# Convolution layer in another order, pairs read by halves, products nobody reads, and one root for a double norm

## The chip, the cores and the metric

The kernel runs on 1 core of one Trainium2 chip. The metric is the device time of one execution in microseconds, the median of the runs shown. It was measured three times before the change.

## The reference, cut to what matters

A residual stream x of 256 tokens by 1024 features (fp32) goes through six layers, each a mixer and a feed-forward part, with an RMS norm ahead of each of them:

```python
for i in range(4):                       # retention, conformer convolution, stick breaking, retention
    x = x + mixer_i(rms_norm(x, norm_mix[i]))
    x = x + squared_relu_mlp(rms_norm(x, norm_ffn[i]), ffn_w1[i], ffn_w2[i])
x = rms_norm(x, final_norm)              # together with the next one: a double norm
for layer in range(2):                   # hybrid layers
    h = rms_norm(x, g_mix[layer])
    ...
return rms_norm(x, g_final)
```

The convolution mixer is `h = a * sigmoid(gate)` from one projection, a causal depthwise convolution of 31 taps over time for each of the 1024 channels, a layer norm over the channels, silu, and a projection. The retention mixer projects q, k, v and a gate; q and k are normed over each head of 256 features, rotated, and used for decayed scores over the 256 tokens. `rms_norm(x, w) = x * rsqrt(mean(x*x) + 1e-6) * w`.

## The kernel before, in words

Weights stream through two buffers of 2 MB ("units" of 128 x 4096 fp32, loaded by SyncE in two pieces of 1 MB; unit u is loaded when unit u-1 has been split). ScalarE rounds each piece to fp32r (`w_hi`, L1327), VectorE takes the rest (`w_lo`, L1926), and TensorE makes every product of three: high by high, high by low, low by high (`three`, L778 to L780; `unit_both`, L807 and L810, does it in two). The activations (`act_hi`, `act_lo`, `hid_hi`, `hid_lo`) are split in the same way. Every engine walks the same list of units in an order written out by hand, and semaphores tie the engines together.

Results go to two PSUM `pair`s of 1024 columns (two banks each), used in turn: `open_pair` waits until the use before the last was drained, by ScalarE or VectorE, which signal `drained`. The residual sums of the output projections go to a third PSUM region, `acc`.

**Retention** (`retention` on each engine). Four units make q and k by tokens (`unit_t`: the product of tokens 0 to 127 into the pair's first bank, of tokens 128 to 255 into its second; each unit has two pieces, so the first bank is complete at three quarters of the unit). ScalarE copies the whole pair (L1549), takes four sums of squares (L1553), evacuates the turned pair before (`rotate_evac`, L1544), takes the root (`roots`); VectorE norms and rotates (L2199 to L2210) and signals `qk_ready`; TensorE turns the result (`transposes`, L944). Per head a unit makes v, which ScalarE copies whole into `R_V` (L1570), scores (L1003) follow, then a gate unit, and the weighted sum (L1011 to L1013).

**Convolution layer** (`conformer`). Four units give h; ScalarE adds biases and takes the sigmoid (L1597, L1600), VectorE multiplies two tiles of 128 channels each (`gated(i)`, L2321, which signals `conv_gated`). Tiles 0 and 1 are convolved on VectorE, 31 taps by two tiles, 62 instructions (L2301, L2304), with the other work of VectorE put between them by `between`. Tiles 2 to 7 (`STACKED_TILES`) are convolved on TensorE (`convolve(n)`, L1029, 32 products each, in four groups of 32 columns) from copies shifted in time: GpSimd (`stack_tiles`) stores two tiles of h to `u_rows` in HBM (L669), waits for the landing, and gathers each tile back with four DMAs (L676) into one of four buffers. Tiles 6 and 7 use the buffers of tiles 2 and 3 again, so GpSimd waits for `squared` before it gathers them. The channel mean is first estimated from tiles 0 and 1 (`C_NEG`, L1042 on TensorE, L1624 on ScalarE) and taken off every tile (L2346, L2331); the exact mean and variance come by products with `C_MEAN` (L1047 to L1055), the last of which need tile 7. L1639, L1640, L2364, L1642 and L2371 to L2376 make the normed values, L1651 the silu, L1385 and L1979 the split, and the output projection starts (`unit_r`, L778).

```python
gated(0)
convolve(0, 1, {4: second_piece, 14: lambda: gated(1), 15: lambda: ahead(CONV_FIRST + 3), 27: lambda: gated(2)})
gated(3)
```

**Norms** (`norm`, on ScalarE and VectorE). Per half a of the tokens and half n of the columns VectorE adds the residual (L2014), multiplies by the gain row (`by_row`, L2006), ScalarE squares with a running sum (L1417), VectorE adds and inverts (L2020, L2021), ScalarE takes the root (L1400) and scales (L1406), TensorE turns the half (`turn_half`, L848), inside the first unit for a = 1. Ahead of hybrid layer 0 (`row=True`) the norm is double: after the first root ScalarE writes x back, normed with the row `final_norm` (L1406, `x<-work`), then the second gain, the second sum, the second root and the second scaling follow for the same half.

**Start and end.** At the start x, the identity and the first weights are loaded, normed (`norm_first`) and turned. At the end VectorE scales each half of the tokens (L2740), and GpSimd stores it as one DMA of 512 KB (L736).

## Time and profile before

| what | value |
|---|---|
| median of 3 runs | 2360.89 us (2360.59 to 2361.51) |
| the profiled execution, its own time | 2362.6 us |
| its span, first to last instruction | 2360.8 us |
| mean granted TensorE clock in it | 0.996 |
| HBM read, written | 430.73 MB, 6.16 MB; 185 GB/s over the span |

The rows further down are from the profiled execution, in microseconds from its first instruction. A timeline row reads: start, duration, engine, line, operation, output <- input, shape, count, and in brackets how long the engine had been idle before it and what released it. Ends of matmuls are modelled (a matmul's duration holds its way through the array), so the pace of TensorE is read from start to start. Equal instructions that follow each other are merged into one row with a count.

### The profile page before, as it was taken

How to read it: one execution, taken by the hardware profiler on the slowest of the kernel's cores; microseconds unless marked ns; L12 is line 12 of the kernel's file. 1: busy time of each engine (PE TensorE's matmuls, PEld its weight loads, DVE VectorE, ACT ScalarE, POOL GpSimd, SP SyncE). 2: the span in 40 equal slices, each digit the busy share in tenths (PEclk: the TensorE clock that was granted, in tenths of full speed). 3: DMA queues.
4: the chain of work that ended last, by engine and by line, in shares of the span. 5: the costliest groups of instructions: out<-in, count | busy, mean ns of one | idle time of the engine just before them, and what ended most of it. 6: DMA issues, size and time to landing. Idle time of an engine off the chain costs nothing.

```text
span 2360.8 us, 31036 instructions
## 1 busy us (share of the span) xinstructions
PE 2311.3 (98%) x12362; PEld 1933.3 (82%) x12362; DVE 1571.2 (67%) x1650; ACT 1211.9 (51%) x1347; POOL 86.1 (4%) x136
## 2 busy tenths in 40 slices
PE   8999999889999999999999999999999999999998
PEld 6788888678888788877788877888888887888887
DVE  7666676766567765686576567867655667677555
ACT  5545445354356644464454365544644656446444
POOL 0000030200000000000000000000000000000000
PEclk9999999999999999999999999999999999999999
DMA  7454654634443355545454544445454544454543
GB/s 272 185 173 178 246 201 191 203 112 188 187 179 155 139 199 213 196 161 191 183 201 178 189 176 176 168 161 200 180 196 178 216 178 173 161 192 182 197 174 128
DMA packets 71848, 434.21 MB, mean 184 GB/s; under 512 B 11648, under 2 KB 11968, under 8 KB 26176
## 3 DMA queue, kind: packets, MB, share of 16 engines
q1 hardware_dynamic: 59184, 399.78, 44.2%
q0 software_dynamic: 12560, 32.96, 4.5%
q8 instruction: 75, 1.23, 0.2%
q14 instruction: 29, 0.24, 0.0%
HBM read 430.73 MB, written 6.16 MB: 185 GB/s over the span
## 4 chain that ended last, share of the span: by engine, by line
PE 93%; DVE 4%; ACT 2%; issue 1%; DMA 0%; POOL 0%; DVEq 0%; ACTq 0%
PE pair L807 21%; PE pair L810 11%; PE acc L778 10%; PE acc L779 10%; PE acc L780 10%; PE pair L778 6%; PE pair L780 5%; PE pair L779 5%; PE pair L819 4%; PE pair L820 2%; PE pair L1029 1%; DVE work L2304 1%; DVE w_lo L1926 1%; PE pair L848 1%; PE acc L1206 1%
## 5 line engine op out<-in xcount | busy, mean ns | idle before, releaser
L1926 DVE TENSOR_TENSOR w_lo<-raw,w_hi 128x2048 fp32r<-128x2048 f32 (+1 forms) x402 | 865.0, 2173 | 112.4 <-ACT w_hi L1327 108.6
L1327 ACT ACTIVATE w_hi<-raw 128x2048 fp32r<-128x2048 f32 (+1 forms) x402 | 717.0, 1805 | 53.7 <-PE acc L780 47.9
L807 PE MATMUL pair<-act,w_hi 128*128 128x512 f32 x1920 | 602.7, 395 | 0.0
L810 PEld LDWEIGHTS pair<-act,w_lo 128*128 128x128 f32 x1920 | 360.6, 188 | 84.8
L810 PE MATMUL pair<-act,w_lo 128*128 128x256 f32 x1920 | 377.3, 278 | 0.0
L778 PE MATMUL acc<-w_hi,hid 128*128 128x512 f32 x848 | 333.9, 394 | 0.0
L779 PE MATMUL acc<-w_lo,hid 128*128 128x512 f32 x848 | 330.4, 390 | 0.0
L780 PE MATMUL acc<-w_hi,hid 128*128 128x512 f32 x848 | 330.2, 389 | 0.0
L807 PEld LDWEIGHTS pair<-act,w_hi 128*128 128x128 f32 x1920 | 295.5, 189 | 3.6
L1472 ACT ACTIVATE gate<-pair 128x512 f32<-128x512 f32 x104 | 62.2, 598 | 458.2 <-PE pair L810 435.8
L2116 DVE TENSOR_TENSOR gate<-pair,gate 128x512 f32<-128x512 f32 x104 | 71.7, 690 | 255.0 <-ACT gate L1472 254.6
L778 PE MATMUL pair<-w_hi,act 128*128 128x512 f32 (+1 forms) x576 | 228.0, 396 | 5.1 <-DVE act L1979 2.7
L780 PE MATMUL pair<-w_hi,act 128*128 128x512 f32 (+1 forms) x576 | 222.2, 386 | 0.0
L779 PE MATMUL pair<-w_lo,act 128*128 128x512 f32 (+1 forms) x576 | 222.1, 386 | 0.0
L780 PEld LDWEIGHTS acc<-w_hi,hid 128*128 128x128 f32 x848 | 159.2, 188 | 33.6
L778 PEld LDWEIGHTS acc<-w_hi,hid 128*128 128x128 f32 x848 | 159.2, 188 | 33.2 <-issue 1.9
L779 PEld LDWEIGHTS acc<-w_lo,hid 128*128 128x128 f32 x848 | 159.2, 188 | 32.0 <-issue 1.4
L819 PE MATMUL pair<-act,w_hi 128*128 128x512 f32 x448 | 162.2, 403 | 0.0
L778 PEld LDWEIGHTS pair<-w_hi,act 128*128 128x128 f32 x576 | 108.8, 189 | 32.5 <-issue 9.5
L780 PEld LDWEIGHTS pair<-w_hi,act 128*128 128x128 f32 x576 | 108.7, 189 | 22.1
L779 PEld LDWEIGHTS pair<-w_lo,act 128*128 128x128 f32 x576 | 108.8, 189 | 20.6 <-issue 0.7
L820 PE MATMUL pair<-act,w_lo 128*128 128x256 f32 x448 | 125.5, 280 | 0.0
(273 smaller groups left out, 2671.9 us busy)
## 6 DMA issues: line engine op xcount, KB each, us to landing
raw<-weights SPq DMA_DIRECT2D x354, 1024.0 KB, 6.7
raw<-weights SPq DMA_DIRECT2D x52, 512.0 KB, 4.0
work<-bias_scratch POOLq DMA_DIRECT2D x32, 192.0 KB, 2.7
val<-gains POOLq DMA_DIRECT2D x11, 512.0 KB, 4.0
bias_scratch<-bias_rows POOLq DMA_DIRECT2D x4, 1024.0 KB, 19.9
hid<-u_rows POOLq DMA_DIRECT2D x20, 142.0 KB, 3.4
work<-ret_gn_w POOLq DMA_DIRECT2D x8, 256.0 KB, 5.3
work<-ret_gn_b POOLq DMA_DIRECT2D x8, 256.0 KB, 5.8
```

The lines of the kernel that those rows point to most:

```text
L778: mm(o, a_hi, b_hi, start=start, stop=False)
L779: mm(o, a_hi, b_lo, start=False, stop=False)
L780: return mm(o, a_lo, b_hi, start=False, stop=stop)
L807: mm(tiles(o[:, 512 * n:512 * n + 512]), h[:, k, n * P:(n + 1) * P], both[:, :, k, :], start=k == 0, stop=False)
L810: last = mm(o[:, 512 * n:512 * n + SEQ], l[:, k, n * P:(n + 1) * P], both[:, 0, k, :], start=False, stop=k == KT - 1)
L819: mm(tiles(o[:, b:b + 512]), h[:, k, cs], both[:, :, k, :], start=k == 0, stop=False)
L820: last = mm(o[:, b:b + SEQ], l[:, k, cs], both[:, 0, k, :], start=False, stop=k == KT - 1)
L848: last = tr(o[:, P * k:P * (k + 1)], xs[:, a, P * k:P * (k + 1)], ident[:])
L1327: run(w_hi[slot][:, part], raw[slot][:, part], ACT.Copy).then_inc(hi_done, 1)
L1472: run(tiles(dst), o[:].rearrange("p (n h t) -> p n h t", n=2, h=2)[:, :, 1, :], ACT.Copy).then_inc(gate_ready, 1)
L1926: tt(w_lo[slot][:, part], raw[slot][:, part], w_hi[slot][:, part].bitcast(F32), ALU.subtract).then_inc(lo_done, 1)
L2116: return tt(tiles(dst), o[:].rearrange("p (n h t) -> p n h t", n=2, h=2)[:, :, 0, :], tiles(low), ALU.add).then_inc(done, 1)
```

## The change

It has five parts.

1. Retention: `unit_t` and `first_unit` signal `token_half` when the first bank of the pair is complete. ScalarE copies that bank (and, for q and k, squares it) then, and the second bank after the unit. `roots(4)` comes ahead of `rotate_evac(i - 1)`. The v pairs are copied in the same two halves.
2. Convolution layer: `gated(1)`, the split of unit `CONV_FIRST + 3`, `gated(2)` and `gated(3)` stand at taps 6, 9, 14 and 28 of VectorE's convolution (before: 14, 15, 27 and behind it). The split of unit `CONV_FIRST + 4` comes behind the convolution, not ahead of `gated(3)`. TensorE convolves tiles 2, 3 and 4 at once, takes the mean estimate from tiles 2 and 3, and then convolves tiles 5, 6 and 7; ScalarE evacuates tiles 2 to 4 with their bias; `C_NEG` is taken off five tiles in one instruction. GpSimd waits for `drained` in place of `squared`. Tile 6 enters the exact mean by the sum on VectorE. `C_DSQ` is made ahead of `C_DELTA`, and VectorE waits for it alone.
3. Products that nobody reads (`keep_busy`, fp32, 128x128x128, into a part of `acc` that is written anew afterwards): 18 ahead of the first load's wait, 12 behind the first turn, 24 behind the last variance product of the convolution layer.
4. Double norm: `both_inverses` gives both roots at once from two sums of squares: with s1 the mean square of x and s2 that of x*row, the first root is 1/sqrt(s1+eps), both together 1/sqrt(eps*(s1+eps)+s2). The gain is multiplied on at once; x itself is scaled at the end of `norm` on VectorE.
5. End: VectorE scales the first 512 columns, ScalarE the other 512, and SyncE stores each quarter (256 KB) as soon as it is ready, in place of two DMAs of GpSimd.

The diff, cut to its core:

```diff
@@ sync @@
+            for a in range(2):
+                for n in range(2):
+                    sp.wait_ge(out_ready[n], a + 1)
+                    sp.dma_start(out[P * a:P * (a + 1), wide(n)], xs[:, a, wide(n)]).then_inc(out_stored, 16)
+            sp.wait_ge(out_stored, 64)
@@ gpsimd @@
                         if n >= 4:
-                            pool.wait_ge(squared, n - 2)
+                            p = CONV_PAIR + n - 4
+                            pool.wait_ge(drained[p % 2], p // 2 + 1)
...
-            for a in range(2):
-                pool.wait_ge(x_ready, x_signals - 3 + 3 * a)
-                pool.dma_start(out[P * a:P * (a + 1), :], xs[:, a, :]).then_inc(stored, 16)
-            pool.wait_ge(stored, 112)
@@ tensor @@
+                        if by_half and (piece, a) == (1, 0):
+                            last.then_inc(token_half, 1)
...
+            def keep_busy(m, n):
+                for _ in range(n):
+                    mm(IDLE, m, m, start=True, stop=True)
...
-                pe.wait_ge(conv_ready, 2)
+                uses = [convolve(n) for n in range(3)]
+                assert uses[0] == CONV_PAIR
+                await_drained(uses[1])
                 o = open_pair()
-                for k in range(2):
-                    last = mm(o[:, 0:SEQ], C_MEAN, C_Y[:, k, :], start=k == 0, stop=k == 1)
+                for k in (2, 3):
+                    last = mm(o[:, 0:SEQ], C_MEAN, C_Y[:, k, :], start=k == 2, stop=k == 3)
                 last.then_inc(pair_full, 1)
-                uses = [convolve(n) for n in range(len(STACKED_TILES))]
+                uses += [convolve(n) for n in range(3, 6)]
                 o = open_pair()
                 pe.wait_ge(summed, 1)
...
-                for k in (6, 7):
-                    await_drained(uses[k - 2])
...
+                await_drained(uses[5])
+                mm(o[:, 0:SEQ], C_MEAN, C_Y[:, 7, :], start=False, stop=True).then_inc(mean_ready, 1)
+                pe.wait_ge(squared, 4)
+                mm(o[:, 512:512 + SEQ], C_MEAN, C_SQ[:, 7, :], start=False, stop=True).then_inc(pair_full, 1)
+                keep_busy(ident[:], 24)
...
+            pe.wait_ge(warm_in, 1)
+            keep_busy(WARM, 18)
             pe.wait_ge(loaded, 16)
             first_half()
+            keep_busy(ident[:], 12)
@@ scalar, norm @@
                     if row:
-                        times_root(a, x, x_ready)
+                        for n in range(2):
+                            square_of(x, a, n, 2 * a + n)
+                            last = square_of(BY_ROW, a, n, 4 + 2 * a + n)
+                        last.then_inc(ss_ready, 1)
+                        act.wait_ge(rinv_ready, S.due("rinv_ready"))
+                        link(run(rstd[:, 2 * a:2 * a + 2], rinv[:, 2 * a:2 * a + 2], ACT.Sqrt))
+                        for n in range(2):
+                            run(xs[:, a, wide(n)], xs[:, a, wide(n)], ACT.Copy,
+                                scale=rstd[:, 2 * a:2 * a + 1]).then_inc(xs_ready, 1)
+                    else:
                         square(a, 0)
                         square(a, 1)
-                    times_root(a, xs, xs_ready)
+                        times_root(a, xs, xs_ready)
@@ scalar, retention @@
                 for i in range(4):
-                    next_unit()
+                    ahead(S.u + 1)
                     o, done, slot = use()
-                    run(xs[:, i % 2, :], o[:], ACT.Copy).then_inc(done, 1)
...
+                    for a in range(2):
+                        if a == 0:
+                            await_half()
+                            link(run(xs[:, i % 2, wide(a)], o[:, wide(a)], ACT.Copy))
+                        else:
+                            unit_end()
+                            run(xs[:, i % 2, wide(a)], o[:, wide(a)], ACT.Copy).then_inc(done, 1)
+                            await_drained(S.p - 1)
+                        for g in (2 * a, 2 * a + 1):
...
                     last.then_inc(ss_ready, 1)
+                    roots(4)
                     if i:
                         rotate_evac(i - 1)
-                    roots(4)
@@ scalar, conformer @@
+                for k in (2, 3, 4):
+                    o, done, _ = use(False)
+                    await_pair()
+                    run(C_Y[:, k, :], o[:, 0:SEQ], ACT.Identity, bias=colv("dw_b", k)).then_inc(done, 1)
...
+                square(0, 5)
+                for k in (5, 6, 7):
                     use(False)
                     await_drained(S.p - 1)
                     square(k)
+                    if k < 7:
+                        split_piece(S.u + 1, k - 5)
...
+                run(C_DSQ, o[:, 0:SEQ], ACT.Square).then_inc(delta_ready, 1)
                 run(C_DELTA, o[:, 0:SEQ], ACT.Copy).then_inc(delta_ready, 1)
@@ scalar, end @@
+                root(a).then_inc(last_root, 1)
+                act.wait_ge(last_root, a + 1)
+                run(xs[:, a, wide(1)], xs[:, a, wide(1)], ACT.Copy, scale=rstd[:, a:a + 1]).then_inc(out_ready[1], 1)
@@ vector @@
+            def both_inverses(a):
+                whole, first = rinv[:, 2 * a:2 * a + 1], rinv[:, 2 * a + 1:2 * a + 2]
+                dve.wait_ge(ss_ready, S.due("ss_ready"))
+                link(stt(first, ss[:, 2 * a:2 * a + 1], EPS, ss[:, 2 * a + 1:2 * a + 2], ALU.add, ALU.add))
+                link(stt(whole, first, EPS, ss[:, 4 + 2 * a:5 + 2 * a], ALU.mult, ALU.add))
+                link(tt(whole, whole, ss[:, 5 + 2 * a:6 + 2 * a], ALU.add))
+                nc.vector.reciprocal(rinv[:, 2 * a:2 * a + 2], rinv[:, 2 * a:2 * a + 2]).then_inc(rinv_ready, 1)
...
+                            tt(BY_ROW[:, a, wide(n)], x[:, a, wide(n)], ROW[:, wide(n)], ALU.mult).then_inc(x_ready, 1)
+                            dve.wait_ge(x_ready, S.due("x_ready"))
+                            by_row(a, n, gain, BY_ROW)
...
+                if row:
+                    for a in range(2):
+                        link(ts(x[:, a, :], BY_ROW[:, a, :], rstd[:, 2 * a + 1:2 * a + 2], None, ALU.mult))
@@ vector, conformer @@
                 gated(0)
-                convolve(0, 1, {4: second_piece, 14: lambda: gated(1), 15: lambda: ahead(CONV_FIRST + 3),
-                                27: lambda: gated(2)})
-                gated(3)
+                convolve(0, 1, {4: second_piece, 6: lambda: gated(1), 9: lambda: ahead(CONV_FIRST + 3),
+                                14: lambda: gated(2), 28: lambda: gated(3)})
+                ahead(CONV_FIRST + 4)
...
+                five_y = C_Y[:, 0:5, :]
+                tt(five_y, five_y, C_NEG.unsqueeze(1).broadcast_to([P, 5, SEQ]), ALU.add).then_inc(centred, 1)
...
                 o, done = fetch_pair()
-                dve.wait_ge(delta_ready, 2)
+                dve.wait_ge(delta_ready, 1)
@@ vector, start and end @@
+            nc.vector.memset(WARM, 0.0).then_inc(warm_in, 1)
...
-                await_roots()
-                ts(xs[:, a, :], xs[:, a, :], rstd[:, a:a + 1], None, ALU.mult).then_inc(x_ready, 1)
+                dve.wait_ge(last_root, a + 1)
+                ts(xs[:, a, wide(0)], xs[:, a, wide(0)], rstd[:, a:a + 1], None, ALU.mult).then_inc(out_ready[0], 1)
```

## Rows read from the trace of the kernel before

**Rows 1.** The page, busy time of the engines: us, share, instructions.
```profile
PE 2311.3 (98%) x12362; PEld 1933.3 (82%) x12362; DVE 1571.2 (67%) x1650; ACT 1211.9 (51%) x1347; POOL 86.1 (4%) x136
```

**Rows 2.** The waits of PE: line waited, releaser: us in total, times, longest.
```profile
PE acc L778 <- DVE act L1979: 6.4, 1, 6.4
...
PE pair L1003 <- ACT work L1570: 3.9, 8, 1.2
```

**Rows 3.** Timeline of PE in retention 0: start, us, instruction, xcount [idle before <-releaser].
```profile
36.04 1.03 PE L944 MATMUL pair<-ident,work 128*128 128x128 f32 x8
37.31 0.50 PE L778 MATMUL pair<-w_hi,act 128*128 128x512 f32 x1 [0.24 <-ACT work L1549]
...
70.35 0.39 PE L780 MATMUL pair<-w_hi,act 128*128 128x512 f32 x1
70.83 1.09 PE L944 MATMUL pair<-ident,work 128*128 128x128 f32 x8
71.67 0.48 PE L778 MATMUL pair<-w_hi,act 128*128 128x512 f32 x1
```

**Rows 4.** Chain that ended last: start, us, what.
```profile
61.19 1.03 ACT work L1549
```

**Rows 5.** Groups by form, ACT, 444 to 494: busy, mean ns, idle.
```profile
L1385 ACT ACTIVATE act<-val 128x512 fp32r<-128x512 f32 x4 | 2.5, 630 | 0.1
```

**Rows 6.** Timeline of DVE in the convolution layer.
```profile
435.05 9.59 DVE L2304 SCALAR_TENSOR_TENSOR work<-work,cols 128x256 f32<-128x256 f32 x24
...
448.45 4.49 DVE L1926 TENSOR_TENSOR w_lo<-raw,w_hi 128x2048 fp32r<-128x2048 f32 x2
452.86 0.69 DVE L2321 TENSOR_TENSOR work<-work,gate 128x512 f32<-128x512 f32 x1
```

**Rows 7.** Timeline of PE in the convolution layer.
```profile
433.08 0.35 PE L778 MATMUL pair<-act,w_hi 128*128 128x256 f32 x1 [0.73 <-DVE w_lo L1926]
...
448.59 1.91 PE L1042 MATMUL pair<-work 128*128 128x256 f32 x4 [3.77 <-DVE work L2304]
...
461.68 3.63 PE L1029 MATMUL pair<-val,work 128*32 128x256 f32 x64
...
469.60 8.61 PE L1029 MATMUL pair<-hid,work 128*32 128x256 f32 x128 [4.29 <-issue]
...
479.97 0.59 PE L1051 MATMUL pair<-work 128*128 128x256 f32 x2
...
480.40 0.59 PE L1055 MATMUL pair<-work 128*128 128x256 f32 x2
...
487.35 0.77 PE L778 MATMUL acc<-w_hi,act 128*128 128x512 f32 x1 [6.35 <-DVE act L1979]
```

**Rows 8.** One line's view, L669, the three stores of u_rows.
```profile
DMA to landing us min/median/max: 2.9/3.2/9.9
```

**Rows 9.** Windows: length, busy PE PEld DVE ACT POOL, clock, DMA share, GB/s.
```profile
488.00:492.00 4.00, 4.00 (x11) 3.17 (x10) 3.21 (x5) 3.94 (x10) 0.00 (x0) 0.50 0.00 0
...
500.00:510.00 10.00, 10.00 (x46) 8.24 (x45) 7.58 (x9) 6.05 (x9) 0.00 (x0) 1.00 0.47 199
```

**Rows 10.** Timelines of ACT and PE, double norm before hybrid layer 0.
```profile
1385.07 1.34 ACT L1406 ACTIVATE x<-work,small 128x512 f32<-128x512 f32 x2
...
1388.29 1.33 ACT L1406 ACTIVATE work<-work,small 128x512 f32<-128x512 f32 x2
...
1389.07 0.66 PE L848 MATMUL pair<-ident,work 128*128 128x128 f32 x4 [2.28 <-ACT work L1406]
```

**Rows 11.** Timeline of PE at the start.
```profile
11.43 0.76 PE L778 MATMUL pair<-w_hi,act 128*128 128x512 f32 x1 [2.69 <-DVE act L1979]
...
15.37 0.40 PE L778 MATMUL pair<-w_hi,act 128*128 128x512 f32 x1
```

**Rows 12.** Timelines of DVE and POOL at the end.
```profile
2354.59 0.75 DVE L2740 TENSOR_SCALAR work<-work,small 128x1024 f32<-128x1024 f32 x1 [0.27 <-ACT small L1400]
...
2355.64 0.54 POOL L736 DMA_DIRECT2D out<-work  x1 [3.56 <-DVE work L2740]
```

116 lines of the change are left out of this document (58 added, 58 removed).

## The prediction

> **What bounds the kernel now.** I read the page first: TensorE is busy 98% of the span [rows 1], so apart from fewer products only its waits and its half-speed stretches can be won. TensorE's waits come next [rows 2], then the timeline around each. They fall into five places, one for each part of the change. Durations are from the profiled execution (2362.6 us, span 2360.8); its own time is 1.7 above the median of the runs, 2360.89, and I take the sum off the median.
>
> **Retention, by halves.** After a unit TensorE turns the rotated pair before, and then needs the pair that ScalarE is copying. From the start of the turn to the next product are 1.27 us where it waits (36.04 to 37.31) and 0.84 where it doesn't (70.83 to 71.67) [rows 3]: 0.43 is lost, though the idle column says 0.24. The copy of 1024 columns takes 1.03 [rows 4], one of 512 0.63 (the nearest form, also out of PSUM) [rows 5]. With the first bank copied during the unit's last quarter, the pair is free 0.40 earlier, just about when the turn is through. There are five such places for q and k (the row at 37.31 is the first), and eight for v, where TensorE waits 3.9 in all [rows 2]: two of them wait 1.21, and keep 0.8. So 13 x 0.40 = 5.2. `qk_ready` is late too: the product at 70.35 should be followed after 0.23 but the turn starts 0.48 later [rows 3]; now the squares of the first bank lie under the unit, and the sums are ready over 1 us earlier. 2 x 0.25 = 0.5. Sum 5.7. What the part adds: an extra fixed cost of two ScalarE copies per unit (2 x 0.63 against 1.03, so 0.2) and a wait at three quarters of the unit; behind that wait on ScalarE stands only what before stood behind the end of the unit, since the split of the next unit comes ahead of both. `rotate_evac` slips about 0.8 behind the root, and is needed a unit later. Bounds: 0 (ScalarE reading one bank slows the products into the other; nothing here shows it) and 6.5.
>
> **Convolution layer.** Before: the fourth unit ends at 444.8 (448.59 less 3.77), TensorE waits for VectorE's last tap, makes the mean estimate, convolves four tiles, waits 4.29 for the gathered tiles, and starts the output projection at 487.35 [rows 7].
> VectorE first. A tap instruction takes 0.40 (9.59 for 24), a split pair 4.4 (448.45 to 452.86) [rows 6]. VectorE has no gap here, so positions can be shifted by sums: the last `gated` moves ahead of six taps (2.4) and of a split pair (4.4), from 452.86 to 446.1. `gated(2)` moves from tap 27 to 14, to about 434.5. The last tap ends at 449.2, the split pair at 453.6. The split that made TensorE wait 0.73 at 433.08 [rows 7] now comes ahead, five taps earlier: the unit ends 0.8 earlier, at 444.0.
> TensorE: a tile takes 3.5 at full clock (3.63 for tile 5, modelled end included). Tiles 2 to 4: 444.0 to 454.5, two mean products of 0.43 (479.97 to 480.40) to 455.4, tiles 5 to 7 to 465.9 [rows 7].
> Is what it needs there? `C_NEG` at 456, five tiles at once on VectorE (some 1.5) and three sums to about 459.3, the squares' sums to 461.5: tile 5's drain at 459.4 comes 3 us ahead of tile 7's need of that pair. `summed` is made near 464, ahead of 465.9. The third store is issued at 446.9 rather than 453.8. The three stores landed after 2.9, 3.2 and 9.9 us [rows 8]; the slow one went out just behind 2 MB of weights. At 446.9 the weights of the unit before have landed and the next are asked for at 453.6, so I take 3.2: gathers from 450.2, one per 0.55, the last at 454.1. With about 3.5 to land they are there by 457.6, against 462.4 when tile 7 needs its buffer. The weights then in flight touch only the last gather.
> The end: four statistics products to 467.7; the projection starts 6.5 behind their end before (480.83 to 487.35), now 6.2, as the squares are made first: 473.9. That is 13.4 earlier than 487.35.
> The clock: from 488 to 492 it is granted at 0.50, 1.2 GHz, with 11 records (nine starts) in 4 us; later 1.00, 2.4 GHz, with 46 in 10 us (0.227 each) [rows 9]. It had fallen in the 6.35 us of idleness before 487.35. The 24 dummy products are 128 columns, half of 0.43, so 0.22 each: 5.2 us, from 467.7 to 472.9, a microsecond ahead of need. So they cost nothing, and the idleness left is 1 us. At half speed from 487.35 to at least 492, at most 494, half of it was lost: 2.3 to 3.3, I take 2.8. Sum 13.4 + 2.8 = 16.2. Bounds: 11 (a stall of up to 5, below) and 17.5.
>
> **A rule against the trace.** The weights ride on SyncE's queue, the stores and gathers on GpSimd's, and the third store took three times as long beside weights [rows 8]. The Trainium skill, "DMA: Bandwidth & Descriptors", section "SWDGE vs HWDGE vs iDMA", says that a DMA engine goes round robin between such queues, by which a store of 0.3 MB would get its share beside the weights and land long before them. By that rule no placement here costs a stall, and the last two gathers are safe; the row says otherwise, and I keep the stall as a rival.
>
> **Double norm.** ScalarE's first scaling starts at 1385.07, the second at 1388.29, and TensorE's turn follows at 1389.07 after 2.28 of idleness [rows 10]. The pass between the scalings, 3.2 us, goes. The new chain adds per half a product (0.69), a square (0.6) and two tiny instructions (0.4); but VectorE, rid of the second pass of a = 0, starts a = 1's residual 1.1 us earlier, and the first product of the unit comes 1.1 earlier too. My walk has the second turn at 1385.9, 3.2 earlier, with 0.5 of idleness left. The scaling of x at the end (2 x 0.75, the price of L2740 [rows 12]) delays the split behind it by 0.6 against its cover, ScalarE's rounding; TensorE needs that split 0.7 later. If that cover were gone it would cost 0.6. I take 3.2; bounds 2 and 4.
>
> **Start.** The first product runs at 11.43, and until 15.37 products start 0.43 apart instead of 0.23 [rows 11], the pace of the half clock. The 18 dummies start at about 1.0, at half speed at first, and end between 6.4 and 7.7; the first turn was at 6.8. At full clock the first products outrun VectorE's splits, which then gate them: my walk gives 0.7. Bounds: a loss of 1 (the dummies delay the turn) and a gain of 1.5.
> The Trainium skill, "TensorE: Matmul & The Clock Gate", Part 1, says that the number of slow products at a kernel's start differs from run to run; by it the same 18 would sometimes be too many, within those bounds.
>
> **End.** The last scaling starts at 2354.59 and takes 0.75, GpSimd's issue follows at 2355.64 [rows 12]. Halves on two engines save 0.3 for a = 0 and 0.1 for a = 1, and SyncE can issue without the 0.3 that lay between the scaling (ended 2355.34) and GpSimd's row: 0.7. Bounds: 0 and 2, since a smaller last store may also land sooner. The skill's DMA page above, "Anatomy of one DMA", has 2.0 us fixed plus the bytes at 436 GB/s, an estimate of 0.6 less for 256 KB than for 512; by it the sum would be 0.6 lower.
>
> **Sum.** 5.7 + 16.2 + 3.2 + 0.7 + 0.7 = 26.5; 2360.9 - 26.5 = 2334.4. Behind these places the MLP stages are all TensorE, and VectorE's splits run ahead there, so what is won stays won.
>
> **Rivals.**
> *The clock doesn't hold* (the dummies are too few or come too late): the 2.8 and the start's 0.7 are gone, 2337.9. For it: the half clock held 4 us and more under real work [rows 9]. Against it: only 1 us of idleness is left. 0.12.
> *The gathers stall*: the third store lands as late as before (9.9): gathers from 456.9 to 460.8, tile 6 waits 3.6, and the clock may fall once more, 1.7: 2339.7. For it: rows 8. Against it: no weights in flight at 446.9. 0.15.
> *The halves give nothing*: ScalarE reading beside TensorE's writes, or coming late to its wait: 2340.1. 0.08.
> *Slower than before*: the clock falls ahead of the layer's convolutions, and their short products of 32 columns don't bring it back, so that 21 us of tiles, 2.6 of statistics, 5.2 of dummies and 21.8 of projection all take twice as long, 50 us more: 2384. It decides once more than 26.5 us of full-speed work runs at half speed. Against it: tiles 6 and 7, 6.9 us at full clock, took 8.6 after a gap of 4.29 [rows 7], so these products do bring the clock back. 0.03.
> *The change doesn't do what it says* in its largest part: no such case, the order is written out.
>
> **The numbers.** As forecast 0.62, its own range 2331 to 2337. The range for 8 in 10 takes in clock and gathers: 2330 to 2340. A measurement of this kernel can tell about 0.2%, 4.7 us. Faster by more 0.95, within it 0.02, slower 0.03.
>
> **What would show it.** Right: TensorE's waits on L1549 and L1570 shrunk to two of about 0.8; tile 5, 6 and 7 without a gap; a granted clock of 1.00 through the projection; one wait of about 0.5 at the double norm. Wrong: an idle time of over 1 us ahead of tile 6 or 7, 0.50 behind the dummies, the dummies ending later than VectorE's first `act_lo`, or the first turn later than 6.8.

## The result, and the profile after

The changed kernel takes 2347.39 us (median of 4 runs, 2345.64 to 2349.41), against 2361.2 for the kernel before on the same chip: a ratio of 0.9937, 95% interval 0.9922 to 0.9952. It is faster by 13.8 us; 26.5 were forecast, and the time lies outside the range. The sign was right, the size was off by half, and most of what is missing is in one place.

The two profiled executions (spans 2360.8 and 2346.5) differ by 14.3 us. The table reads them stage by stage, as the shift of the same instruction between the two timelines of TensorE. The forecast for retention, 5.7 for both layers, is split by its places: 2.65 in retention 0 and 3.05 in retention 1.

| part | forecast | found |
|---|---|---|
| start and retention 0 (last turn before the layer: 411.16, now 410.87) | 3.35 | 0.29 |
| convolution layer, start of its projection (487.35, now 484.38) | 13.4 | 2.68 |
| the clock behind it (projection to the next norm's product: 204.90, now 202.45) | 2.8 | 2.45 |
| retention 1 | 3.05 | 2.38 |
| double norm | 3.2 | 3.64 |
| end (start of the last product to the end of the span: 10.12, now 7.26) | 0.7 | 2.86 |
| sum | 26.5 | 14.3 |

The page's busy times, which answer to [rows 1]. TensorE now stands for 29 us of its span instead of 50. It has 104 records more: 108 of the products that nobody reads (54, two records each), less 4 of the statistics, so part of the busy time is theirs:

```profile
PE 2317.8 (99%) x12466; PEld 1943.3 (83%) x12466; DVE 1571.9 (67%) x1654; ACT 1215.9 (52%) x1359; POOL 85.4 (4%) x134
```

The waits of TensorE (line waited for, us in total, times, longest), against [rows 2]. The wait of 6.4 ahead of the projection is gone, and the eight for the v pair (now L1023) are two of 0.8, as forecast. At the head stands a wait that was 4.3 before: the taps (now L1049), released by "issue", that is, by nothing that the engines' records name.

```profile
PE pair L1049 <- issue: 7.8, 2, 6.8
...
PE pair L1023 <- ACT work L1618: 1.6, 2, 0.8
PE pair L789 <- DVE w_lo L1977: 1.5, 2, 1.2
PE pair L789 <- DVE w_lo L2094: 1.2, 1, 1.2
```

Where it stands shows in the timeline of TensorE in the convolution layer, against [rows 7]. Everything that the engines do runs as forecast: tile 2 at 443.51 (forecast 444.0), no wait for the mean estimate, and 6.37 us from the end of the last statistics product to the projection (forecast 6.2). But tile 4 waits 1.06 and tile 6 waits 6.78:

```profile
443.51 7.11 PE L1049 MATMUL pair<-hid,work 128*32 128x256 f32 x128
451.68 3.66 PE L1049 MATMUL pair<-hid,work 128*32 128x256 f32 x64 [1.06 <-issue]
...
466.77 9.48 PE L1049 MATMUL pair<-hid,work 128*32 128x256 f32 x128 [6.78 <-issue]
...
478.01 5.52 PE L859 MATMUL acc<-ident 128*128 128x128 f32 x48
484.38 0.47 PE L789 MATMUL acc<-w_hi,act 128*128 128x512 f32 x1 [0.85 <-DVE act L2030]
```

The wait of 6.78 costs more than itself. Tiles 6 and 7 then take 9.4 us (466.77 to the first statistics product at 476.18) where they need 7.0 at full clock (a tile is 3.47 from start to start, 453.63 to 457.10 in hold_all below). The windows of 2 us show the granted clock (busy PE with its records, clock, DMA share, GB/s): half at first, full later. That is another 2.4 us.

```profile
468.00:470.00 2.00, 2.00 (x24) 0.50 0.00 0
474.00:476.00 2.00, 2.00 (x44) 1.00 0.00 0
```

Tiles 4 and 6 wait for gathers, so the next view is GpSimd's queue in the same stretch. VectorE had the second and third pairs gated at 434.7 and 446.5. The second store goes out at once, at 435.07, but GpSimd then waits 10.38 us for it to land. The third store stands in the same queue behind that wait and behind eight gathers, and goes out at 450.52, not at 446.9:

```profile
423.48 0.74 POOL L683 DMA_DIRECT2D u_rows<-work  x1 [65.25 <-DVE work L2390]
430.10 4.39 POOL L691 DMA_DIRECT2D hid<-u_rows  x8 [5.88 <-DMA u_rows<-work]
435.07 0.72 POOL L683 DMA_DIRECT2D u_rows<-work  x1 [0.57 <-DVE work L2390]
446.17 2.19 POOL L691 DMA_DIRECT2D hid<-u_rows  x4 [10.38 <-DMA u_rows<-work]
448.35 2.18 POOL L691 DMA_DIRECT2D val<-u_rows  x4
450.52 0.72 POOL L683 DMA_DIRECT2D u_rows<-work  x1
455.35 0.57 POOL L691 DMA_DIRECT2D hid<-u_rows  x1 [4.10 <-DMA u_rows<-work]
```

What lay beside it is on SyncE: the weight loads, two DMAs of 1 MB each time, issued when the unit before has been split. The change also moved one of them, since the split of unit `CONV_FIRST + 3` now stands at tap 9 and not at 15: VectorE is through with it at 430.09 instead of 435.13. The load that went out at 435.32 before goes out at 430.27; the one after it stays (453.40, before 452.97). SyncE before, then after:

```profile
435.32 0.86 SPq L556 DMA_DIRECT2D raw<-weights  x2
```

```profile
430.27 0.86 SPq L565 DMA_DIRECT2D raw<-weights  x2
...
453.40 0.82 SPq L565 DMA_DIRECT2D raw<-weights  x2
```

The time from issue to landing, the three stores (L683) and then the 24 gathers (L691), against [rows 8]:

```profile
DMA to landing us min/median/max: 4.5/6.3/10.8
```

```profile
DMA to landing us min/median/max: 3.1/8.0/11.1
```

Before, they were 2.9/3.2/9.9 and 2.7/3.5/9.6. The order of time says more. The eight gathers issued from 430.10, beside the load of 430.27, take 5.2 to 11.1; the eight from 446.17, with no weights in flight, 3.1 to 3.9; the eight from 455.35, beside the load of 453.40, 7.6 to 9.4. The stores take 6.3, 10.8 and 4.5. Before the change five gathers took over 5 us, now sixteen do.

In retention 0, VectorE's first head norm waits 4.84 us for a table that it doesn't use (2.69 before, when TensorE had no wait behind it); TensorE now waits twice, 1.96 in all. These are the rows of VectorE and TensorE:

```profile
29.84 0.17 DVE L2041 TENSOR_SCALAR small<-small 128x4 f32<-128x4 f32 x1 [4.84 <-DMA work<-table_bucket_hot]
...
36.33 1.09 PE L964 MATMUL pair<-ident,work 128*128 128x128 f32 x8 [0.76 <-DVE work L2278]
38.62 0.47 PE L789 MATMUL pair<-w_hi,act 128*128 128x512 f32 x1 [1.20 <-DVE w_lo L1977]
```

The double norm on TensorE, against [rows 10]: the wait of 2.28 ahead of the second turn is 0.17, and from the start of the unit's last product (1370.29, before 1378.15) to the second turn there are 7.42 us instead of 10.92. The other wait in this stretch, ahead of the unit's first product, is 1.62 and was 1.90.

```profile
1370.52 1.03 PE L866 MATMUL pair<-ident,work 128*128 128x128 f32 x8
1373.18 0.47 PE L789 MATMUL acc<-w_hi,act 128*128 128x512 f32 x1 [1.62 <-issue]
...
1377.71 0.66 PE L866 MATMUL pair<-ident,work 128*128 128x128 f32 x4 [0.17 <-ACT work L1496]
```

The end, against [rows 12], VectorE and then SyncE. The last scaling takes 0.49, and a quarter store lands 2.2 us after its issue, where half the output took 2.9:

```profile
2342.88 0.49 DVE L2814 TENSOR_SCALAR work<-work,small 128x512 f32<-128x512 f32 x1 [0.27 <-ACT small L1422]
...
2339.57 4.64 SPq L609 DMA_DIRECT2D out<-work  x4
```

### The profile page after: what moved, and what is told of

Read it like the earlier page. It is cut to its first block, busy times and chain, and to the rows that moved or that the text cites. A ratio compares the mean times of both kernels' runs of the same rounds, so it can differ in the third digit from the quotient of the medians.

```text
span 2346.5 us, 31261 instructions
## 1 busy us (share of the span) xinstructions
PE 2317.8 (99%) x12466; PEld 1943.3 (83%) x12466; DVE 1571.9 (67%) x1654; ACT 1215.9 (52%) x1359; POOL 85.4 (4%) x134
## 4 chain that ended last, share of the span: by engine, by line
PE 93%; DVE 3%; ACT 1%; DMA 1%; issue 1%; SPq 0%; POOL 0%; DVEq 0%; ACTq 0%; POOLq 0%
PE pair L818 22%; PE pair L821 11%; PE acc L789 10%; PE acc L790 10%; PE acc L791 10%; PE pair L789 6%; PE pair L791 5%; PE pair L790 5%; PE pair L830 4%; PE pair L831 2%; DVE w_lo L1977 1%; PE pair L1049 1%; PE pair L964 1%; PE pair L866 1%; PE acc L1225 1%
## 5 line engine op out<-in xcount | busy, mean ns | idle before, releaser
L1507 ACT ACTIVATE gate<-pair 128x512 f32<-128x512 f32 x104 | 62.2, 598 | 457.6 <-PE pair L821 435.4
```

What stands on the lines that cost most here:

```text
L1507: run(tiles(dst), o[:].rearrange("p (n h t) -> p n h t", n=2, h=2)[:, :, 1, :], ACT.Copy).then_inc(gate_ready, 1)
```

## Experiments

The theory after this reading: the convolution layer's gain is eaten by weight loads that share the DMA engines with stores and gathers; hold them back and the forecast's timeline comes true. Rivals: the order in GpSimd's queue (the third store stands behind the second's gathers), or a fixed price of these transfers when they start early. All kernels below are the changed kernel with one edit, unless said otherwise. A view used throughout is the distance from tile 2 to the projection: 36.91 before, 40.87 after, 29.9 in the forecast (444.0 to 473.9).

**hold_both.** The weight loads are held at two places: one until the second store has landed, the next until all gathers have.

```diff
+                if mixer_units == 6:
+                    loads(4)
+                    load()
+                    sp.wait_ge(u_stored, 32)
+                    load()
+                    sp.wait_ge(stacked[1], 128)
+                else:
+                    loads(mixer_units)
```

> The changed kernel, but SyncE issues the sixth unit's load of the convolution layer (at 430.3 in the changed kernel) only when the second store of u_rows has landed, and the load after it (453.4) only when tile 7 is gathered. Theory (weights in flight beside GpSimd's stores and gathers make them late): the second store lands in about 3 us instead of 11, the third goes out at about 446 instead of 450.5, tile 4 waits less than 1, tiles 6 and 7 wait at most 1, the projection starts at 474 to 477 instead of 484.4, and the time is 8 to 11 us below the changed kernel (2336 to 2340). Rival (the stores and gathers are slow by themselves, small packets through GpSimd's queue): the gap of 6.8 ahead of tile 6 stays over 5, the time stays at 2345 to 2349. A second rival (the held loads come too late for the next units): a new wait for w_lo of 2 us or more behind the layer.

Measured: 2340.75 us, ratio to the kernel before 0.9908 (0.9892 to 0.9925), a little outside the 2336 to 2340 expected. The distance falls from 40.87 to 34.80. Stores land after 4.2/6.2/8.1 us: the third, issued at 445.69, ran beside the weights released at 438.18, and tile 6 still waits 2.34 where at most 1 was expected. Holding the load earns 6.1 of the 11 us, and where a load was let go too early, the store beside it was slow again.

**third_store_first.** GpSimd issues the third store ahead of the second store's gathers; the loads are untouched.

```diff
...
+                    if i == 2:
+                        store(3)
+                    if i == 3:
+                        pool.wait_ge(third_stored, 16)
...
```

> The changed kernel, but GpSimd stores the third pair of tiles as soon as the second store has landed and the tiles are ready (about 446.5), ahead of the eight gathers of tiles 4 and 5, not behind them (450.5). Loads are not held. Theory (GpSimd's own order makes the third store late, 4 us of the gap): store at 446.5, gathers of tiles 6 and 7 from about 451, the gap of 6.8 ahead of tile 6 falls to 1 to 3.5; tile 4 waits 0.7 longer. Time 3 to 5 us below the changed kernel. Rival (only the weights issued at 453.4 count): the gathers of tile 7 still run beside them and land when they land, the gap moves to tile 7 and the time falls by under 2.

Measured: 2343.88 us (0.9926, 0.9909 to 0.9942). The store goes out at 444.94, and the wait of 6.78 ahead of tile 6 becomes three waits, here in TensorE's timeline:

```profile
451.49 3.66 PE L1057 MATMUL pair<-hid,work 128*32 128x256 f32 x64 [2.95 <-issue]
...
460.14 3.66 PE L1057 MATMUL pair<-hid,work 128*32 128x256 f32 x64 [0.34 <-issue]
466.33 5.57 PE L1057 MATMUL pair<-hid,work 128*32 128x256 f32 x64 [2.53 <-issue]
```

5.82 together instead of 7.84, and a distance of 38.61. The queue's order is worth about 2 us here, and it isn't clear of the spread: the executions whose loads and stores are those of the changed kernel lie between 37.9 and 41.7, and the intervals of the two ratios overlap. The larger part, by the run above, is the weights'.

**hold_all.** One hold, but for everything: the load that went out at 430.27, and with it the one behind, waits until tile 7 is gathered.

```diff
+                if mixer_units == 6:
+                    loads(4)
+                    load()
+                    sp.wait_ge(stacked[1], 128)
+                    load()
+                else:
+                    loads(mixer_units)
```

> The changed kernel, but both loads that ran beside the stores and gathers (the sixth unit's and the one behind it) are issued only when tile 7 is gathered. In the run that held the sixth only until the second store had landed, the third store still took 8.1 us beside it. Theory (each store and gather beside weights is slow, alone it takes about 3 to 4): the third store goes out at about 446 and lands in 3 to 4 us, tile 6 waits under 0.5 us, and from tile 2's first product to the projection's first are 29.5 to 31 us (40.9 in the changed kernel, 34.8 with the earlier hold); time 2335 to 2338. Against it (GpSimd's own queue is the limit): 33 to 35 us from tile 2 to the projection, as with the earlier hold. The sixth unit then arrives at about 463, which ScalarE's splits between the squares may feel: at most 2 us.

Measured: 2338.04 us (2336.09 to 2339.21; 0.9892, 0.9876 to 0.9909), 9 us below the changed kernel. The distance is 33.25, more than the 29.5 to 31 expected and in the range that was to speak for GpSimd's queue as the limit. Where the time goes decides between them. Stores and gathers from issue to landing:

```profile
DMA to landing us min/median/max: 3.0/4.2/6.2
```

```profile
DMA to landing us min/median/max: 2.7/3.3/4.7
```

The store of 6.2 is the first: it went out at 422.04, behind the load of 419.58, which isn't held. No tile waits, so GpSimd's queue is not the limit, and tiles 6 and 7 run at full clock. Late is now the held weight: ScalarE's splits of it stand between the squares in its program, and the statistics wait for the squares. TensorE's timeline:

```profile
453.63 3.66 PE L1055 MATMUL pair<-val,work 128*32 128x256 f32 x64
457.10 7.09 PE L1055 MATMUL pair<-hid,work 128*32 128x256 f32 x128
...
465.72 0.67 PE L1075 MATMUL pair<-work 128*128 128x256 f32 x2 [1.53 <-DVE work L2438]
...
468.44 0.70 PE L1080 MATMUL pair<-work 128*128 128x256 f32 x2 [1.18 <-ACT work L1659]
```

33.25 less these 2.71 is 30.5, against 29.9 forecast: for the engines the forecast's timeline was right to 0.6 us.

**old_hold.** The kernel before with the same lines of the hold, which asks whether the new order is needed at all. They do more than the expectation below says: its text names one load of those at 452.97, but the load of 435.32 is held too, and SyncE issues both behind each other from 467.24.

> The kernel before, in its own order, with one of the two weight loads that it issues at 452.97 held until tile 7 is gathered. If what the third store pays is the bytes in flight beside it, its landing falls from 9.9 to 5 to 7 us, tile 6 waits 1 us or less where it waited 4.29, and the layer is 3 to 4 us shorter: 2357 to 2358. If one load of 1 MB beside it is enough to hold the store back, it still lands after 9 us or more and the time stays within 1 us of 2361.

Measured: 2366.08 us in a single run (the kernel before: 2362.05). The stores' landing does what the expectation said, and more; the time doesn't follow. The stores' landing, then ScalarE, then TensorE:

```profile
DMA to landing us min/median/max: 2.9/3.3/4.3
```

```profile
472.06 1.91 ACT L1333 ACTIVATE w_hi<-raw 128x2048 fp32r<-128x2048 f32 x1 [11.55 <-DMA raw<-weights]
...
478.46 1.22 PE L1053 MATMUL pair<-work 128*128 128x256 f32 x2 [5.21 <-DVE work L2337]
```

The distance is 38.48, 1.6 more than before the hold. Tile 6's wait of 4.29 is gone, and the statistics wait 5.21, since in this order the gathers end 10 us later (last one issued at 463.7, not 453.0) and so does the released load. The expectation stopped at the wait it removed and didn't ask what is late next. This hold pays only together with the early gathers that the new order allows. A hold of the load of 452.97 alone, which is what the expectation describes, was not run on the old order, so whether a shorter hold would have paid there stays open.

**no_24.** Without the 24 products behind the statistics.

```diff
-                keep_busy(ident[:], 24)
```

> The changed kernel without the 24 products behind the variance product. Theory (they keep the clock up over 6.4 us of idleness): the granted clock is 0.50 behind the start of the projection, its first products start 0.43 apart for 4 to 6 us, and from the projection's start to the first product behind the next norm (484.38 to 686.83 in the changed kernel, 202.45 us) it takes 2.3 to 3.2 us longer. The projection itself starts at the same distance behind the last statistics product. Rival (the clock would stay up without them): no difference.

Measured: 2347.61 us in a single run. TensorE stands for 6.20 us ahead of the projection, which at first runs at 1.2 GHz. The windows (length, busy PE with its records, granted clock, DMA share, GB/s):

```profile
480.00:485.00 5.00, 3.53 (x9) 0.53 0.00 0
485.00:490.00 5.00, 5.00 (x24) 1.00 0.32 105
```

From the projection to the next norm's product there are 203.68 us against 202.45: the 24 products are worth 1.23, half of what was expected. Of the projection 3.2 us ran at half clock here (481.47 to about 484.7, from the 0.53 of the window) and 5.8 in the kernel before (487.35 to about 493.2: [rows 9], and 0.71 in the window of 492 to 494), after nearly the same idle time (6.20 and 6.35). The total hides the loss, for this execution's distance was 38.88, 2 us shorter than after's.

**no_start.** Without the 18 and the 12 products of the start.

```diff
-            pe.wait_ge(warm_in, 1)
-            keep_busy(WARM, 18)
             pe.wait_ge(loaded, 16)
             first_half()
-            keep_busy(ident[:], 12)
```

> The changed kernel without the 18 and the 12 products at the start. Theory: as before the change, first product near 11.4, the next ones 0.43 apart until about 15.4, and the whole first unit ends 0.3 to 1 us later than in the changed kernel. Rival (the first unit is bound by VectorE's splits and the turn anyway): less than 0.3. In five executions with the products the first turn started between 6.9 and 8.0 (6.8 before the change), so they can cost up to 1 us as well.

Measured: 2344.29 us in a single run, 3 below the changed kernel, but not for this reason: its distance is 37.94. From the first product to the scores of head 0 it takes 63.01 us, against 62.2 to 62.9 (median 62.28) in the seven executions with them where TensorE had no wait behind the table; its first product starts at 11.70, and in twelve executions with them at 11.37 on average (10.84 to 12.10). So one run without them puts their worth at about 1 us (0.3 + 0.7), less than the spread of the rest. The 18 products took 5.7 to 7.2 us, and the slow ones hold up the first turn: where they took 7.0 or more, it started at 7.9 to 8.1 and the first product at 11.9 to 12.1, later than in the kernel before.

**rope_apart.** The rotation table and the two gains get a semaphore of their own, so that VectorE's head norm no longer waits for the bucket table issued with them.

> The changed kernel, but the rotary table and the two norm rows have a semaphore of their own, so that VectorE's first rotation doesn't wait for the decay table, rel_bias and bucket_hot. Theory (retention 0's gain went into this wait): VectorE's first L2041 starts at about 26.3 instead of 29.84, the waits of TensorE of 0.76 at 36.33 and 1.20 at 38.62 are gone, and the row at 76.01 comes 1.8 to 2.6 us earlier. Rival (VectorE would have been held by something else, ScalarE's sums or the split): under 1 us.

Measured: 2348.14 us in a single run. VectorE starts its head norm at 26.87, after 1.38 of idleness that no table ends any more, and the two waits of TensorE are gone: first product to head 0 62.28 (after 65.02, before 64.46). The total shows nothing of it, as the distance was 41.65. With the shared semaphore the wait is a matter of luck, as the other executions of the new order show: where the head norm started by 27.9 TensorE didn't wait, and where it started at 28.3 to 29.8 it waited 0.8 to 2.0.

**turned_shared.** Ahead of each head's gate unit ScalarE copies one bank of the turned pair and VectorE the other.

```diff
...
+                            await_pair()
+                            run(val[:, S.c % 2, wide(0)], o[:, wide(0)], ACT.Copy).then_inc(half_copied, 1)
...
```

> The changed kernel, but the turned gated pair of a head is copied by ScalarE (first bank) and VectorE (second bank) and not by VectorE alone (1.22 us, begun behind a weight split). Theory (the 0.43 won per head at the v pair is given back, since the gate unit waits for this copy): the distance from the turn to the gate unit (2.51 us in the changed kernel, 2.61 before) falls to 2.2 or less in each of the six heads, 2 to 4 us over both retentions. Rival (the gate unit waits for its weights or for the scores): it stays at 2.5.

Measured: 2341.95 us in a single run. From turn to gate unit 2.18 us in each head, where the changed kernel has 2.42 to 2.50 and before 2.61; the stretch from the first scores of retention 1 to the row norm is 320.79 against 321.74. So 0.95 in this layer and at most 1.9 over both, just below the 2 to 4 expected. The rest of the 5 us is a shorter distance (38.41) and an early table.

**whole_copies.** The changed kernel with q, k and v copied whole, as before.

> The changed kernel with the retention's q, k and v copied whole again by ScalarE, as before, and all else as changed. My theory after the trace (the halves take 0.4 off the wait for the turn, and what a head wins is given back at its gate unit, which waits for VectorE's copy): 0.1 to 0.2 per head and a little at the layers' ends, so 2 to 3 us lost: 2349.5 to 2350.5, and from the first scores of retention layer 1 to the row norm 323.6 us as in the kernel before, against 321.7. Rival: the halves give nothing, and the 1.8 us that the second retention stretch gained come from elsewhere: the stretch stays at 321.7 and the time at 2347.

Measured: 2349.57 us in a single run. In retention 1, norm to first scores takes 62.25 against 60.35, and first scores to row norm 322.39 against 321.74: the halves are worth 1.90 + 0.65 = 2.55 in that layer, of 3.05 forecast. The time came out as expected by luck, since this execution's distance was 39.06, 1.8 shorter than the changed kernel's. The place did not come out (323.6 in the second stretch): three quarters of the worth is in the q and k units.

**pool_stores.** The same four quarter stores, issued by GpSimd.

```diff
...
+                    pool.wait_ge(out_ready[n], a + 1)
+                    pool.dma_start(out[P * a:P * (a + 1), wide(n)], xs[:, a, wide(n)]).then_inc(out_stored, 16)
...
```

> The changed kernel, but its four stores of the result are issued by GpSimd and not by SyncE. Before the change 10.1 us lay between TensorE's last product and the end of the span, in the changed kernel 7.3. Theory (the tail behind the last byte belongs to GpSimd's way of issuing and ending, 2.4 us against 0.4): about 9.5 to 10.3. Rival (the halves and the smaller last store made the gain): it stays at 7.3 to 8.

Measured: 2349.45 us in a single run; start of the last product to the end of the span 10.07, as before (10.12), not 7.26. The DMA share in 40 slices of 2339 to 2349, the changed kernel and then this one. The bytes are through in slice 27 of the one (by 2345.75, span 2346.5) and slice 23 of the other (by 2344.75, span 2347.7):

```profile
DMA  0000029999920000000019999940000000000000
```

```profile
DMA  0699298500000000399489700000000000000000
```

So the end's gain is neither the scaling nor the smaller store, for both are in this kernel: behind the last byte some 2.9 us pass where GpSimd issued it and 0.8 where SyncE did. That is 2.1 of the 2.8; the rest lies ahead of the last byte.

**best_after_gathers and best_after_store.** Both have the hold, rope_apart and turned_shared in one, and ScalarE's two splits of the held weight each one square later. They differ in what releases the load; the diff goes from the first to the second.

```diff
-                    sp.wait_ge(stacked[1], 128)
+                    sp.wait_ge(u_stored, 48)
```

> The changed kernel with everything that paid so far: the last weight load that falls beside the gathers waits until tile 7 is gathered; the rotation table and the gains of the first retention layer have a semaphore of their own, so that VectorE doesn't wait for tables it doesn't read yet; the turned pair of each head is copied half by ScalarE and half by VectorE; and ScalarE's two splits of the late weight stand one square later. My theory (each of these is a wait of its own that adds up): 2338.0 of the run with the hold alone, less 2 x 0.95 for the shared copies, about 1 for the tables and 1.0 to 1.5 for the square that no longer stands behind a split: 2333.5 to 2335. The statistics of the convolution layer then wait 0.5 or less where they waited 1.53. Rival: the parts hide one another and the late split only moves to the next square, so that the wait before the last statistics product grows from 1.18 to 2.5: 2336 or more.

> The same, but the held weight load waits only for the landing of the third store, so that it runs beside the last gathers. If the gathers suffer beside a weight load whatever holds the queue (they took 8.0 and 11.1 us in the changed kernel beside weights and 3.1 to 3.7 without), the last two gathers land 4 to 5 us later, tile 6 waits 1 to 2 us and tile 7 up to 3, and the kernel is 1 to 4 us slower than with the longer hold. Rival: only a store suffers, since it reads SBUF in long rows beside the weights' writes; then the gathers keep 3 to 4 us, the sixth unit is split before the squares need ScalarE, and this version is 1 us faster than the other.

Measured, both on the same chip: 2337.04 us (2336.4 to 2337.58; 0.9893, 0.9878 to 0.9908) and 2344.8 us (2343.85 to 2346.01; 0.9927, 0.9913 to 0.994). The held load goes out at 455.60 in the first and at 446.56 in the second. The early release costs 7.8 us, twice the upper end of what was expected. The gathers' landing in it and TensorE at tile 6:

```profile
DMA to landing us min/median/max: 2.9/3.6/16.6
```

```profile
460.71 6.23 PE L1058 MATMUL pair<-hid,work 128*32 128x256 f32 x64 [5.42 <-issue]
```

All stores had landed when the load was released (3.2/4.4/6.6 us, in the other version 3.0/4.0/6.5), so what slowed down is gathers of 142 KB alone, up to 16.6 us beside four loads of 1 MB, and the rival by which only stores suffer has fallen.

The fast one fell short of its forecast (2333.5 to 2335), and its rival was right in the sum: the wait only moved, though to another place. Its statistics have no wait any more, but from their last product to the projection there are 9.35 us, from start to start, instead of the 6.80 of the changed kernel, as ScalarE's second split of the late weight now stands ahead of the copies of the mean. And TensorE, idle for 3.40 us of it, starts the projection at half the clock. Row of TensorE, and the window around it, whose mean clock of 0.77 is 1.00 up to the projection and 0.50 from there:

```profile
472.75 0.76 PE L798 MATMUL acc<-w_hi,act 128*128 128x512 f32 x1 [3.40 <-DVE act L2041]
```

```profile
470.00:475.00 5.00, 2.25 (x5) 0.77 0.02 5
```

**best_longer_cover.** The same with 36 products on the identity instead of 24.

> The version with all the fixes, with 36 products on the identity instead of 24 behind the statistics. In that version the last of the 24 ended at 469.35, TensorE then stood for 3.40 us, and the projection began at half the clock (0.63 us a product, for 3 us): its stretch up to the next norm took 203.78 us against 202.45 in the changed kernel. 12 more at 0.23 us fill 2.8 of the 3.4 us. My theory, by which the idle time ahead of the projection is what brings the clock down: 1.3 us faster, 203.78 back to 202.45, and a time of 2335.5 to 2336. Rival: the low clock has another cause (the stretch of small products in the taps before it): the projection starts at 0.63 us again and the time stays at 2337.

Measured: 2337.25 us (2336.32 to 2337.96; 0.9895, 0.9879 to 0.9912). In the trace the theory holds: 0.89 idle, projection at full pace, and 202.46 us behind it instead of 203.78.

```profile
473.93 0.47 PE L798 MATMUL acc<-w_hi,act 128*128 128x512 f32 x1 [0.89 <-DVE act L2041]
```

But the time did not move, against the forecast of 1.3: this execution's first product started at 12.10 instead of 11.07, which alone is 1.0, and the four runs of either kind spread over 1.2 and 1.6. Whether the median would show it with more runs is open.

## Why the prediction was wrong, and where it was right

**The step that failed** is in the convolution layer: "The third store is issued at 446.9 rather than 453.8", and with it "At 446.9 the weights of the unit before have landed and the next are asked for at 453.6, so I take 3.2: gathers from 450.2". It has three faults.
1. It asked what lies beside the third store and not beside the second. In the kernel before, the second store goes out at 445.66, 10 us behind a load (435.32). The change moves the store to 435.07 and, by the earlier split, the load to 430.27, which the prediction did not see. The store now lands after 10.8 us instead of about 3.2.
2. GpSimd's queue was not followed step by step. The third store stands behind the wait for the second's landing and behind its gathers, so it was issued at 450.52, with its data ready since 446.5. third_store_first puts what that alone cost at about 2 us.
3. "The weights then in flight touch only the last gather" is wrong: with the third store 3.6 late, all eight gathers behind it run beside the loads of 453.40 and need 7.6 to 9.4 us.

Together they lengthened the distance to 40.87 where 29.9 was forecast: 7.8 are the waits of tiles 4 and 6, 2.4 the half clock that the long wait left behind for tiles 6 and 7. hold_all takes the weights away and gets 33.25, or 30.5 without the wait that the late weight itself brings. That is the cause, shown from both sides: with the loads released 9 us earlier (best_after_store against best_after_gathers) 7.8 us are lost again. Not run was the new order with the split left at tap 15, so how much of the loss comes from the load that moved and how much from the store that moved stays open.

**The rival "the gathers stall"** named the mechanism and a time of 2339.7, but at a chance of 0.15 and with the wrong transfer: it had the third store land after 9.9, and that one took 4.5. Slow were the second store and sixteen of the 24 gathers, and tile 6 waited 6.78, not 3.6. Its second term, the clock that falls once more, was 1.7 and came to 2.4. The argument against it, "no weights in flight at 446.9", held for that instant and not for the queue ahead of it.

**The rule against the trace.** Beside weights the stores landed after up to 10.8 us and the gathers after up to 16.6; behind the hold none took over 4.7 (hold_all). The Trainium skill, "DMA: Bandwidth & Descriptors", section "SWDGE vs HWDGE vs iDMA", says that a DMA engine goes round robin between such queues; read as a fair share of bytes, as I read it, the trace disagrees, and it was right not to let it into the sum. How the engines really divide their time no run here shows.

**Retention.** The forecast had 5.7 for both layers. whole_copies prices the halves at 2.55 in retention 1, of 3.05; the mechanism holds, and so do the two waits of 0.78 that stay. In retention 0 the same part gave almost nothing in total, as VectorE, now early, ran into the landing of a table (1.96 of TensorE's waits): the sum with "13 x 0.40" did not ask what is late next. rope_apart takes that wait away and first product to head 0 falls to 62.28, 2.2 below before.

**The clock.** 2.8 forecast, 2.45 found, and 202.45 is, to 0.05, the value of every execution whose idle time ahead of the projection was 0.8 to 2.0 us; with 3.40 and 6.20 it was 203.78 and 203.68. Right in mechanism, and in size against the kernel before (old_hold, in the old order, loses 2.5 there again). But no_24, with nearly the same idle time, puts the products themselves at only 1.23, so the size hangs on how long the low clock lasts.

**Double norm.** 3.2 forecast, 3.50 found at its place (10.92 to 7.42) and 3.64 in the whole stretch. Right. The residual wait was 0.17, forecast 0.5, and behind the scaling of x TensorE shows no wait.

**Start.** The 18 products ended at 6.7; the first turn, released by VectorE, started at 7.00 instead of 6.79. In all twelve executions it started between 6.9 and 8.1, later than the 6.8 that the prediction had named as a sign of being wrong. The real products then outran VectorE's split (1.19 of wait), as forecast. Gained 0.44 by the first product in this execution. Over all of them the bounds (a loss of 1, a gain of 1.5) held: the latest first product was at 12.10 against 11.43 before. The Trainium skill, "TensorE: Matmul & The Clock Gate", Part 1, has the number of slow products at the start differ from run to run, and the traces agree: the same 18 took 5.7 to 7.2 us.

**End.** 0.7 forecast, 2.86 found. The term left out is who issues the store: pool_stores, with all else of the change, gives the whole 2.8 back.

## What to carry to other kernels

When a producer moves earlier, redo the DMA schedule as carefully as the engines': for each transfer that moves, list what is in flight from other queues at the new time, and whether the change moves those too, and follow the issuing queue with its own waits. A load that nobody needs soon may be worth holding until the small transfers that somebody does need have landed, but ask what the held load makes late in turn, and on which in-order engine that stands. In single executions compare stage by stage, since landings and the clock at the start moved these totals by 2 to 4 us, as much as most of the edits.

## What the runs showed of the hardware

- Small transfers beside weight loads: a gather of 142 KB landed after 2.6 to 4.8 us behind the hold (hold_all, best_after_gathers), up to 11.1 with two loads of 1 MB in flight (the changed kernel) and up to 16.6 with four (best_after_store). A store of 287 KB took 2.9 to 4.4 us with none in flight, 6.2 to 6.8 when it was issued some 2 us behind a load, and up to 10.8.
- The end of a store depends on who issued it: about 2.9 us from the last byte to the end of the span with GpSimd, 0.8 with SyncE, for the same four stores (one execution of pool_stores).
- Idle times of TensorE and the clock behind them: after 2.00 us (best_after_store) it stayed at 1.00. After 3.40 us (best_after_gathers) it was granted at 0.50 for about 3 us. After 6.78 us (the changed kernel) two tiles took 9.4 us instead of 7.0, and after 2.34 us (hold_both) 8.7. After 6.20 us (no_24) and 6.35 us (the kernel before) the slow stretch under work was 3.2 and 5.8.
- With loads, stores and gathers in the same order, the layer took 37.9 to 41.7 us from tile 2 to the projection in seven executions: where transfers collide, the loss itself varies.
